# The opening of a two-block transformer kernel: the values' projection in sweeps, its squares summed on VectorE, the constants loaded later, products of ones in front

## The chip, the cores and the metric

The program runs on one core of a Trainium2 chip, as one launch. The metric is the device time of that core in microseconds (us), the median of several runs. The engines are named as the profile names them: PE is TensorE's matrix products and PEld its weight loads, DVE is VectorE, ACT is ScalarE, POOL is GpSimd, SP is SyncE, which here only issues transfers.

## What is computed

Two transformer blocks over 512 tokens of width 1024, one after the other. Cut to what matters here:

```python
# first block; x is (512, 1024)
h = x * rsqrt(mean(x * x, axis=-1) + 1e-6) * pre_norm_g
proj = h @ w_in                      # 3592 columns; v_c are columns 2560 to 3071
q_a, f_a, i_a, g_a, u_b, g_b, q_c, k_c, v_c, g_c, f_c = split(proj)
# a gated recurrence on (q_a, f_a, i_a, g_a), a windowed mean on (u_b, g_b),
# attention with forgetting on (q_c, k_c, v_c, g_c, f_c)
x = x + rmsnorm(concat(o_a, o_b, o_c) @ w_out, post_norm_g)
# second block: two attentions, a merge, an output projection, then a 1024 -> 4096 -> 1024 MLP
```

The root mean square of x is applied after the products: the kernel multiplies the raw x (times the gain) with the weights, and scales the results by token when the sum of squares is there.

## The kernel before

**Two parts of every number.** Each large product is made of three products of rounded numbers. A feature tile x is split into a high part `hh` (ACT, by `enter` at L891) and a low part `hl` (DVE, `enter` at L1294); a weight chunk is split into `wh` (ACT, `hi` at L883) and `wl` (DVE, `lo` at L1289). PE adds hh·wh, hh·wl and hl·wh.

**The stream of weights.** All weights come as chunks of 128 by 1024 in the order of `PLAN`. Each chunk c lands in one of two buffers `raw`, and is split into one of three pairs `wh`, `wl`. SP issues the load of chunk c after `lo(c - 2)` has freed the buffer; `hi(c)` waits until PE is done with chunk c - 3 (`gemm`). The first four chunks, 0 to 3, are the weights of the values v_c (`w1v`), the next is `w1f`, the next two are `w1q`.

**The opening.** SP loads the eight feature tiles in pairs (`load_x`), alternating with chunks 0 and 1, then the constants `con` and `msk`, then chunk 2 and so on. ACT makes for each tile k the high part and, behind it, the square (L894, into `acc` or one of four buffers `S`); POOL adds the squares up into `acc` (L1881), and from tile 5 on ACT's square waits for the addition that frees its buffer. DVE makes the low parts of tiles and chunks in the same order. PE's first program (L457 to L459) takes tile after tile, and in each the four banks `PB0` to `PB3` with three products each: 8 tiles by 4 banks by 3 parts, 96 products of 128 by 512 in all. It waits for `lo` of the chunk and for `xl` of the tile before any of a tile's twelve products. Behind them PE makes the product of chunk 4, in its middle the sums of squares over the partitions (`sums`, L369, four products of one column), and chunks 5 and 6.

**Order on the engines.** The order of every engine is written out by hand in its program. Behind the eight tiles, ACT has a small exponential (L1000) that waits for a DVE operation (L1413), which stands behind all of DVE's low parts of tiles; only then come `hi` and `lo` of chunks 2 to 5. ACT waits for `con` behind `hi(5)`, DVE behind `lo(5)`. The rest of the kernel is driven by PE's progress: its loads and splits are released as PE finishes chunks.

Of the kernel before, what the change touches and what calls it, by code (L numbers as in the profile page):

```python
# [7 lines left out]
F32 = mybir.dt.float32  # L8
# [3 lines left out]
ALU = mybir.AluOpType  # L12
# [29 lines left out]
NW = 1024  # L42
NR, FAR = 2, 8
ORDER1 = (4, 5, 6, 2, 3, 0, 7, 1)

# [118 lines left out]
def build(nc, A, out):  # L164
    with ExitStack() as ctx:
# [144 lines left out]

        SQX = [S[k][:] if k < 4 else ar(12288 + 512 * (k - 4), 512) for k in range(8)]
        half_of = [slice(256 * x, 256 * x + 256) for x in range(2)]
        POST = {1: P_POST1, 2: P_POSTM, 3: P_POSTF}
# [4 lines left out]
        def pe(e):  # L318
# [126 lines left out]


            got = [tenant(m, "vc", m)[0] for m in range(4)]
            for n in range(4):
                c = CH["w1v", n]
                a, b = wh[c % 3], wl[c % 3]  # L450
                e.wait_ge(*to("lo", c))
                for kk in range(2):
                    k = 2 * n + kk
                    w = slice(512 * kk, 512 * kk + 512)
                    e.wait_ge(*to("xl", 0, k))
                    for m in range(4):
                        e.matmul(got[m][:], hh[:, k, col(m)], a[:, w], start=k == 0, stop=False)  # L457
                        e.matmul(got[m][:], hh[:, k, col(m)], b[:, w], start=False, stop=False)
                        i = e.matmul(got[m][:], hl[:, k, col(m)], a[:, w], start=False, stop=k == 7)  # L459
                i.then_inc(*up("gemm", c))  # L460
# [3 lines left out]
            half(c, 0, bank, hh, hl)  # L464
            e.wait_ge(*to("xa", 0, 7))
            sums(0, 5)
# [236 lines left out]
            half(c, 0, bank, hh, hl)  # L703
            e.wait_ge(*to("xs", 7))
            sums(1, 5)
# [171 lines left out]
        def act(e):  # L877
# [7 lines left out]
            def enter(k):  # L885

                if k % 2 == 0:
                    e.wait_ge(semaphore(f"x{k // 2}"), 16)
                if k == 0:
                    e.wait_ge(semaphore("par"), 16)  # L890
                e.activation(hh[:, k, :], X[:, k, :], ACT.Identity, scale=pcol(P_PRE1 + k)).then_inc(*up("xh", 0, k))  # L891
                if k > 4:
                    e.wait_ge(*to("xa", 0, k - 4))
                e.activation(S[k % 4][:] if k else acc[:], X[:, k, :], ACT.Square).then_inc(*up("xq", 0, k))  # L894

# [96 lines left out]
            enter(0)  # L992
            hi(0)
            enter(1)
            enter(2)
            hi(1)
            for k in range(3, 8):
                enter(k)
            e.wait_ge(*to("lb", 0))
            e.activation(lbx[:, 0:2], lbx[:, 0:2], ACT.Exp).then_inc(*up("le"))  # L1000
            for c in range(2, 6):
                hi(c)
            e.wait_ge(semaphore("con"), 16)
# [280 lines left out]
        def dve(e):  # L1284
            def lo(c):
# [4 lines left out]
                                ALU.subtract).then_inc(*up("lo", c))  # L1290

            def enter(k):
                e.wait_ge(*to("xh", 0, k))
                e.scalar_tensor_tensor(hl[:, k, :], X[:, k, :], pcol(P_PRE1 + k), hh[:, k, :].bitcast(F32),  # L1294
                                       ALU.mult, ALU.subtract).then_inc(*up("xl", 0, k))
# [108 lines left out]
            enter(0)  # L1404
            lo(0)
            enter(1)
            enter(2)
            lo(1)
            for k in range(3, 8):
                enter(k)  # L1410

            e.wait_ge(semaphore("par"), 16)
# [8 lines left out]
            e.tensor_scalar(oml, nlb, -1.0, 1.0, ALU.mult, ALU.add).then_inc(*up("lb", 4))  # L1421
            for c in range(2, 6):
                lo(c)
            e.wait_ge(semaphore("con"), 16)
# [250 lines left out]
            for k in range(1, 8):  # L1675
                e.wait_ge(*to("xq", 1, k))
                if k > 1:
                    e.wait_ge(*to("xs", k - 1))
                e.tensor_tensor(acc[:], acc[:] if k > 1 else SQX[0], SQX[k], ALU.add).then_inc(*up("xs", k))
                if k == 3:  # L1680
                    lo(CH["w2e", 2])
# [164 lines left out]
        def pool(e):  # L1846
# [27 lines left out]
            for g in range(4):  # L1874
                r = rows(g % 2)
                e.dma_start(PWM[r, g // 2, rows(g % 2)], A["pool_w"][g]).then_inc(semaphore(f"pw{g}"), 16)
            for k in range(1, 8):
                e.wait_ge(*to("xq", 0, k))
                if k > 1:
                    e.wait_ge(*to("xa", 0, k - 1))  # L1880
                e.tensor_tensor(acc[:], acc[:], S[k % 4][:], ALU.add).then_inc(*up("xa", 0, k))  # L1881

# [96 lines left out]
        def sync(e):  # L1979
# [19 lines left out]
            load_x(2)  # L1999
            load_x(3)  # L2000
            e.dma_start(con[:], A["con"]).then_inc(semaphore("con"), 16)
            e.dma_start(mskw[:], A["msk"]).then_inc(semaphore("msk"), 16)
            for c in range(2, len(PLAN)):
                load(c)
# [139 lines left out]
```

## Time and profile before

| | us |
|---|---|
| median of 3 runs (1023.38 to 1028.22) | 1024.05 |
| profiled execution, its own time | 1029.89 |
| span of the profiled execution | 1028.4 |
| PE busy | 967.5 |
| DVE busy | 593.5 |
| ACT busy | 425.6 |
| POOL busy | 127.4 |

The profiled execution took 1.5 us outside its span, and 5.8 us more than the median of the runs. Starts of PE's instructions are more telling than their durations: a product's row goes on to a modelled end, and the next one starts before that, so the cost of a product in a full stream is the distance between two starts.

### The profile page before, as it was taken

The numbers are of one execution on the slowest core, as the hardware profiler recorded it, in microseconds if no ns is written. First come the engines' busy times: TensorE is split into PE (matmuls) and PEld (weight loads), VectorE is DVE, ScalarE is ACT, GpSimd is POOL, SyncE is SP. The second block draws the span as 40 slices with busy tenths as digits, with TensorE's granted clock in tenths as the row PEclk, the third lists the DMA queues.
The fourth block names the chain that finished last, engine by engine and source line by source line (L and its number), as shares of the span: only waits on it lengthen the run. The fifth ranks groups of instructions, "written<-read, shape, count | busy, mean of one in ns | idle before, by whom it ended". The sixth has DMA issues, their size and how long they took to land.

```text
span 1028.4 us, 13602 instructions
## 1 busy us (share of the span) xinstructions
PE 967.5 (94%) x5210; PEld 781.2 (76%) x5210; DVE 593.5 (58%) x1066; ACT 425.6 (41%) x812; POOL 127.4 (12%) x123
## 2 busy tenths in 40 slices
PE   5998999999999998999998999999989999999992
PEld 4876877767898775766776889978868888888881
DVE  7368558757748676656654752883244344434445
ACT  5354336245465244545544324463233124214321
POOL 6004102321030000000000213030000000000024
PEclk9999999999999999999999999999999999999997
DMA  5221112112233311211212352263323323332002
GB/s 203 98 83 62 42 63 69 56 42 72 83 103 108 139 41 49 70 43 56 82 42 63 101 185 63 82 225 103 101 63 100 103 85 102 103 94 91 21 1 82
DMA packets 24719, 86.72 MB, mean 84 GB/s; under 512 B 2896, under 2 KB 3600, under 8 KB 24400
## 3 DMA queue, kind: packets, MB, share of 16 engines
q1 hardware_dynamic: 23408, 80.25, 24.2%
q10 hardware_dynamic: 1008, 5.28, 1.3%
q8 instruction: 42, 0.69, 0.3%
q0 software_dynamic: 240, 0.33, 0.1%
q14 instruction: 21, 0.17, 0.0%
HBM read 81.65 MB, written 4.19 MB: 83 GB/s over the span
## 4 chain that ended last, share of the span: by engine, by line
PE 80%; DVE 12%; ACT 5%; issue 2%; DMA 0%; POOL 0%; SPq 0%; DVEq 0%; ACTq 0%
PE PB L323 12%; PE PB L325 11%; PE PB L324 11%; PE PB L871 6%; PE PB L870 6%; PE PB L869 6%; PE PB L515 3%; PE PB L542 3%; DVE wl L1289 2%; PE PB L526 2%; PE PB L835 1%; PE PB L354 1%; PE PB L836 1%; PE PB L837 1%; PE PB L355 1%
## 5 line engine op out<-in xcount | busy, mean ns | idle before, releaser
L323 PE MATMUL PB<-hh,wh 128*128 128x512 f32 x592 | 248.8, 420 | 3.5 <-DVE AR L1695 1.9
L325 PE MATMUL PB<-hh,wl 128*128 128x512 f32 x592 | 232.8, 393 | 0.0
L324 PE MATMUL PB<-hl,wh 128*128 128x512 f32 x592 | 232.2, 392 | 0.0
L1289 DVE TENSOR_TENSOR wl<-raw,wh 128x1024 fp32r<-128x1024 f32 (+1 forms) x93 | 119.2, 1283 | 71.1 <-ACT wh L883 71.0
L323 PEld LDWEIGHTS PB<-hh,wh 128*128 128x128 f32 x592 | 112.0, 189 | 36.5 <-issue 12.4
L324 PEld LDWEIGHTS PB<-hl,wh 128*128 128x128 f32 x592 | 112.2, 190 | 24.1 <-issue 3.6
L325 PEld LDWEIGHTS PB<-hh,wl 128*128 128x128 f32 x592 | 111.7, 189 | 24.7
L883 ACT ACTIVATE wh<-raw 128x1024 fp32r<-128x1024 f32 (+1 forms) x93 | 94.5, 1019 | 62.2 <-PE PB L837 14.2
L1033 ACT ACTIVATE S<-S,sm 128x256 f32<-128x256 f32 (+3 forms) x96 | 50.8, 530 | 129.1 <-DVE sm L1374 92.3
L871 PE MATMUL PB<-gh,wl 128*128 128x512 f32 x256 | 99.6, 389 | 0.0
L869 PE MATMUL PB<-gh,wh 128*128 128x512 f32 x256 | 99.6, 389 | 0.0
L870 PE MATMUL PB<-gl,wh 128*128 128x512 f32 x256 | 99.6, 389 | 0.0
L1289 DVE TENSOR_TENSOR wl<-AR,wh 128x1024 fp32r<-128x1024 f32 x56 | 69.4, 1239 | 47.3 <-ACT wh L883 47.3
L883 ACT ACTIVATE wh<-AR 128x1024 fp32r<-128x1024 f32 x56 | 58.9, 1051 | 67.9 <-PE PB L871 67.9
L1812 DVE TENSOR_TENSOR tmp<-tmp 128x512 f32<-128x512 f32 x32 | 23.2, 725 | 82.1 <-ACT gh L1249 82.1
L1860 POOL TENSOR_TENSOR acc<-acc,tmp 128x512 f32<-128x512 f32 x14 | 19.8, 1414 | 329.4 <-ACT tmp L1274 298.6
L1245 ACT ACTIVATE tmp<-PB 128x512 f32<-128x512 f32 x32 | 19.1, 596 | 95.0 <-PE PB L325 92.8
L869 PEld LDWEIGHTS PB<-gh,wh 128*128 128x128 f32 x256 | 48.0, 188 | 10.0
L870 PEld LDWEIGHTS PB<-gl,wh 128*128 128x128 f32 x256 | 48.0, 188 | 10.0
L871 PEld LDWEIGHTS PB<-gh,wl 128*128 128x128 f32 x256 | 48.0, 188 | 9.9
L1374 DVE CUSTOM_DVE_ANT_0 S<-PB,MK 128x128 f32<-128x128 f32 (+3 forms) x64 | 29.8, 489 | 37.7 <-PE PB L515 37.1
L1835 DVE TENSOR_TENSOR AR<-PB,AR 128x512 f32<-128x512 f32 x24 | 16.6, 692 | 60.5 <-PE PB L871 60.5
(337 smaller groups left out, 1669.5 us busy)
## 6 DMA issues: line engine op xcount, KB each, us to landing
AR<-in_dne SPq DMA_DIRECT2D x32, 512.0 KB, 3.5
AR<-in_upe SPq DMA_DIRECT2D x24, 512.0 KB, 3.5
raw<-in_w2g SPq DMA_DIRECT2D x16, 512.0 KB, 3.4
raw<-in_w1e SPq DMA_DIRECT2D x10, 512.0 KB, 3.4
raw<-in_w1q SPq DMA_DIRECT2D x8, 512.0 KB, 3.5
raw<-in_woab SPq DMA_DIRECT2D x8, 512.0 KB, 3.5
raw<-in_w2e SPq DMA_DIRECT2D x6, 512.0 KB, 3.8
X<-in_xT SPq DMA_DIRECT2D x4, 512.0 KB, 6.5
```

Source lines behind the costliest of these rows:

```text
L323: e.matmul(bank[:], a[:, col(k)], xa[:, k, :], start=k == 0, stop=False)
L324: e.matmul(bank[:], a[:, col(k)], xb[:, k, :], start=False, stop=False)
L325: i = e.matmul(bank[:], b[:, col(k)], xa[:, k, :], start=False, stop=k == 7)
L515: last = e.matmul(bank[b][:, k], query[b], key[b][:, k], start=a == 2, stop=x == parts - 1)
L542: x = e.matmul(bank[rows(b), col(i)], v, PT[b][:, j - lo, :], start=j == lo, stop=j == i)
L869: e.matmul(bank[:], a[:, col(k)], gh[:, k, :], start=k == 0, stop=False)
L870: e.matmul(bank[:], a[:, col(k)], gl[:, k, :], start=False, stop=False)
L871: i = e.matmul(bank[:], b[:, col(k)], gh[:, k, :], start=False, stop=k == 7)
L883: e.activation(wh[c % 3][:, 0:PLAN[c][2]], raw_of(c), ACT.Copy).then_inc(*up("hi", c))
L1033: e.activation(s, s, ACT.Exp, bias=nm, scale=-1.0, accum_out=su).then_inc(*up("exp", a, n, b))
L1289: e.tensor_tensor(wl[c % 3][:, 0:n], raw_of(c), wh[c % 3][:, 0:n].bitcast(F32), ALU.subtract).then_inc(*up("lo", c))
L1374: e.tensor_tensor_reduce(soft(n, b)[:, 0:w], seat["max", a, n, b][:, 0:w], MK[:, T - w:T], -1.0, BIG, ALU.add, ALU.min, scalars(n, b)[0]). ...
```

## The change

The change touches the first thirty-odd microseconds.

- PE starts with fourteen products of `ones` by `ones` (128 by 128, not rounded numbers) into bank 7, as soon as `ones` is written.
- For each tile the twelve products of the values are made in three sweeps over the four banks: first hh·wh, then hl·wh, then hh·wl. The first sweep waits for the two high parts only, the second for the tile's low part, the third for the chunk's low part. The number of these products stays 96.
- Chunk 0 is split in two halves of 512 columns, one for each of its tiles (`first_half` on ACT and DVE).
- ACT makes the high parts of tiles 0 to 7 and of chunks 0 to 2 without squares between them; the squares of tiles 0 to 3 come behind `hi(2)`, those of tiles 4 to 7 behind `hi(3)`, each into a buffer of its own (`SQ0`).
- The seven additions of squares move from POOL to DVE, three behind `lo(2)` and four behind `lo(3)`.
- `hi(2)`, `hi(3)`, `lo(2)` and `lo(3)` move ahead of the small exponential and what goes with it.
- SP issues chunks 2 and 3 ahead of `con` and `msk`.

```diff
@@ pe
+            e.wait_ge(*to("one"))
+            for _ in range(WARM):                      # WARM = 14
+                e.matmul(PB[7][:, 0:128], ones[:], ones[:], start=True, stop=True)
             for n in range(4):
-                e.wait_ge(*to("lo", c))
                 for kk in range(2):
+                    e.wait_ge(*to("xh", 0, k))
+                    e.wait_ge(*(to("hi", c) if n else to("hi", 0, kk)))
+                    for m in range(4):
+                        e.matmul(got[m][:], hh[:, k, col(m)], a[:, w], start=k == 0, stop=False)
                     e.wait_ge(*to("xl", 0, k))
                     for m in range(4):
-                        e.matmul(got[m][:], hh[:, k, col(m)], a[:, w], start=k == 0, stop=False)
-                        e.matmul(got[m][:], hh[:, k, col(m)], b[:, w], start=False, stop=False)
-                        i = e.matmul(got[m][:], hl[:, k, col(m)], a[:, w], start=False, stop=k == 7)
+                        e.matmul(got[m][:], hl[:, k, col(m)], a[:, w], start=False, stop=False)
+                    e.wait_ge(*(to("lo", c) if n or kk else to("lo", 0, 0)))
+                    for m in range(4):
+                        i = e.matmul(got[m][:], hh[:, k, col(m)], b[:, w], start=False, stop=k == 7)
@@ act
             enter(0)
-            hi(0)
             enter(1)
+            first_half(0)
+            first_half(1)
             enter(2)
+            enter(3)
             hi(1)
-            for k in range(3, 8):
+            for k in range(4, 8):
                 enter(k)
+            hi(2)
+            for k in range(4):
+                square0(k)
+            hi(3)
+            for k in range(4, 8):
+                square0(k)
             e.wait_ge(*to("lb", 0))
             e.activation(lbx[:, 0:2], lbx[:, 0:2], ACT.Exp).then_inc(*up("le"))
-            for c in range(2, 6):
-                hi(c)
+            hi(4)
+            hi(5)
+            def first_half(x):                         # the one of ACT; dve's is its low part
+                if x == 0:
+                    e.wait_ge(*landed(0))
+                w = slice(512 * x, 512 * x + 512)
+                e.activation(wh[0][:, w], raw_of(0)[:, w], ACT.Copy).then_inc(*up("hi", 0, x))
+            def square0(k):
+                e.activation(SQ0[k], X[:, k, :], ACT.Square).then_inc(*up("xq", 0, k))
@@ dve
+            def added_x(k0, k1):
+                for k in range(k0, k1):
+                    e.wait_ge(*to("xq", 0, k))
+                    if k > 1:
+                        e.wait_ge(*to("xs", 0, k - 1))
+                    e.tensor_tensor(acc[:], acc[:] if k > 1 else SQ0[0], SQ0[k], ALU.add).then_inc(*up("xs", 0, k))
@@ pool
-            for k in range(1, 8):
-                e.wait_ge(*to("xq", 0, k))
-                if k > 1:
-                    e.wait_ge(*to("xa", 0, k - 1))
-                e.tensor_tensor(acc[:], acc[:], S[k % 4][:], ALU.add).then_inc(*up("xa", 0, k))
@@ sync
+            load(2)
+            load(3)
             e.dma_start(con[:], A["con"]).then_inc(semaphore("con"), 16)
             e.dma_start(mskw[:], A["msk"]).then_inc(semaphore("msk"), 16)
-            for c in range(2, len(PLAN)):
+            for c in range(4, len(PLAN)):
                 load(c)
```

On PE, the first rows of its program; before, the first half of the first tile's twelve rows (of the two operands named, the second is the one that is held):

```order
L457 MATMUL PB0<-wh0,hh 128x512
L458 MATMUL PB0<-wl0,hh 128x512
L459 MATMUL PB0<-wh0,hl 128x512
L457 MATMUL PB1<-wh0,hh 128x512
L458 MATMUL PB1<-wl0,hh 128x512
L459 MATMUL PB1<-wh0,hl 128x512
```

Of the change, the same place:

```order
L451 MATMUL PB7<-ones 128x128 x14
L464 MATMUL PB0<-wh0,hh 128x512
L464 MATMUL PB1<-wh0,hh 128x512
L464 MATMUL PB2<-wh0,hh 128x512
L464 MATMUL PB3<-wh0,hh 128x512
L467 MATMUL PB0<-wh0,hl 128x512
L467 MATMUL PB1<-wh0,hl 128x512
L467 MATMUL PB2<-wh0,hl 128x512
L467 MATMUL PB3<-wh0,hl 128x512
L470 MATMUL PB0<-wl0,hh 128x512
```

The first product that needs a chunk's low part is the ninth of a tile now, where it was the second; fourteen products of ones stand ahead.

On DVE, from the low part of chunk 1 on, before (`hl` are low parts of tiles, `wl` those of chunks, the rows on `sm` belong to the small exponential):

```order
L1289 TENSOR_TENSOR wl1<-raw1,wh1 128x1024
L1294 SCALAR_TENSOR_TENSOR hl<-X,par,hh 128x512 x5
L1413 TENSOR_TENSOR sm<-par 128x2
L1415 RECIPROCAL sm<-sm 128x2
L1417 TENSOR_TENSOR sm<-sm 128x2
L1419 TENSOR_TENSOR sm<-sm 128x2
L1421 TENSOR_SCALAR sm<-sm 128x2
L1289 TENSOR_TENSOR wl2<-raw0,wh2 128x1024
```

Of the change, the same place:

```order
L1315 TENSOR_TENSOR wl1<-raw1,wh1 128x1024
L1333 SCALAR_TENSOR_TENSOR hl<-X,par,hh 128x512 x4
L1315 TENSOR_TENSOR wl2<-raw0,wh2 128x1024
L1329 TENSOR_TENSOR acc<-S0,S1 128x512
L1329 TENSOR_TENSOR acc<-acc,S2 128x512
L1329 TENSOR_TENSOR acc<-acc,S3 128x512
L1315 TENSOR_TENSOR wl0<-raw1,wh0 128x1024
L1329 TENSOR_TENSOR acc<-acc,AR 128x512 x4
L1458 TENSOR_TENSOR sm<-par 128x2
```

The low part of chunk 2 comes right behind the last four of the eight tiles, that of chunk 3 behind three additions, and the rows on `sm` behind all seven additions.

## Rows read from the trace of the kernel before

**Rows 1.** The page: busy time, share of the span and instructions of each engine.

```profile
PE 967.5 (94%) x5210; PEld 781.2 (76%) x5210; DVE 593.5 (58%) x1066; ACT 425.6 (41%) x812; POOL 127.4 (12%) x123
```

**Rows 2.** Stages: busy time in each, the granted clock (PEclk), DMA share, GB/s.

```profile
core 0: us, PE busy (x) PEld busy (x) DVE busy (x) ACT busy (x) POOL busy (x), PEclk, DMA share, GB/s
20.00:25.00 5.00, 1.93 (x9) 1.29 (x8) 4.44 (x8) 2.10 (x3) 0.87 (x1) 0.99 0.02 6
25.00:30.00 5.00, 5.00 (x16) 3.94 (x15) 1.29 (x2) 1.06 (x1) 0.00 (x0) 0.67 0.62 204
```

**Rows 3.** Timeline of PE: start, duration, engine, line, out<-in, idle before.

```profile
8.38 0.79 PE L457 MATMUL PB<-wh,hh 128*128 128x512 f32 x1 [8.38 <-DVE wl L1289]
8.98 0.63 PE L458 MATMUL PB<-wl,hh 128*128 128x512 f32 x1
...
11.11 0.47 PE L457 MATMUL PB<-wh,hh 128*128 128x512 f32 x1
...
20.53 0.39 PE L459 MATMUL PB<-wh,hl 128*128 128x512 f32 x1
23.99 0.50 PE L457 MATMUL PB<-wh,hh 128*128 128x512 f32 x1 [3.07 <-DVE wl L1289]
...
28.43 0.40 PE L457 MATMUL PB<-wh,hh 128*128 128x512 f32 x1
...
36.38 0.39 PE L459 MATMUL PB<-wh,hl 128*128 128x512 f32 x1
36.60 0.39 PE L323 MATMUL PB<-hh,wh 128*128 128x512 f32 x1
```

**Rows 4.** Timeline of DVE and POOL in the same stretch.

```profile
5.46 0.75 DVE L1294 SCALAR_TENSOR_TENSOR hl<-X,par,hh 128x512 fp32r<-128x512 f32 x1 [4.45 <-ACT hh L891]
7.11 1.23 DVE L1289 TENSOR_TENSOR wl<-raw,wh 128x1024 fp32r<-128x1024 f32 x1 [0.90 <-ACT wh L883]
8.29 12.58 POOL L1881 TENSOR_TENSOR acc<-acc,S 128x512 f32<-128x512 f32 x7 [1.76 <-ACT S L894]
10.61 2.31 DVE L1289 TENSOR_TENSOR wl<-raw,wh 128x1024 fp32r<-128x1024 f32 x1
12.84 8.58 DVE L1294 SCALAR_TENSOR_TENSOR hl<-X,par,hh 128x512 fp32r<-128x512 f32 x5
```

**Rows 5.** Timeline of ACT in the same stretch.

```profile
4.70 0.72 ACT L891 ACTIVATE hh<-X,par 128x512 fp32r<-128x512 f32 x1 [2.20 <-DMA X<-in_xT]
5.33 0.61 ACT L894 ACTIVATE acc<-X 128x512 f32<-128x512 f32 x1
6.02 1.06 ACT L883 ACTIVATE wh<-raw 128x1024 fp32r<-128x1024 f32 x1
21.53 0.20 ACT L1000 ACTIVATE sm<-sm 128x2 f32<-128x2 f32 x1 [5.57 <-DVE sm L1413]
21.64 1.99 ACT L883 ACTIVATE wh<-raw 128x1024 fp32r<-128x1024 f32 x2
```

**Rows 6.** DMA issues up to 70 us: count, KB each, median us to landing.

```profile
X<-in_xT SPq DMA_DIRECT2D x4, 512.0 KB, 6.5
raw<-in_w1v SPq DMA_DIRECT2D x4, 512.0 KB, 5.6
con<-in_con SPq DMA_DIRECT2D x1, 662.5 KB, 9.5
```

**Rows 7.** The chain that ended last, its piece ahead of the first split of a chunk.

```profile
1.24 4.76 DMA raw<-in_w1v
```

**Rows 8.** Timeline of PE: weight loads and products of numbers that are not rounded.

```profile
39.10 1.08 PEld L369 LDWEIGHTS PB<-ones,acc 128*128 128x128 f32 x8
39.32 0.95 PE L369 MATMUL PB<-ones,acc 128*128 128x1 f32 x8
```

**Rows 9.** Timeline of PE in a later projection with a wait ahead of each sweep.

```profile
259.74 1.07 PE L359 MATMUL PB<-gl,wh 128*128 128x512 f32 x4
260.65 0.39 PE L354 MATMUL PB<-gh,wh 128*128 128x512 f32 x1
```

**Rows 10.** A later stage with a fallen clock, columns as in rows 2.

```profile
80.00:100.00 20.00, 17.13 (x130) 13.01 (x128) 16.94 (x30) 8.34 (x20) 9.89 (x12) 0.91 0.21 73
```

**Rows 11.** The page: the additions of 128 by 512 with both inputs in memory on DVE.

```profile
L1812 DVE TENSOR_TENSOR tmp<-tmp 128x512 f32<-128x512 f32 x32 | 23.2, 725 | 82.1 <-ACT gh L1249 82.1
```

More of the change, by code:

```diff
@@ L43 @@
 NR, FAR = 2, 8
+WARM = 14
 ORDER1 = (4, 5, 6, 2, 3, 0, 7, 1)
@@ L311, in build @@
         SQX = [S[k][:] if k < 4 else ar(12288 + 512 * (k - 4), 512) for k in range(8)]
+        SQ0 = [S[k][:] if k < 4 else ar(2048 + 512 * (k - 4), 512) for k in range(8)]
         half_of = [slice(256 * x, 256 * x + 256) for x in range(2)]
@@ L464, in pe @@
             half(c, 0, bank, hh, hl)
-            e.wait_ge(*to("xa", 0, 7))
+            e.wait_ge(*to("xs", 0, 7))
             sums(0, 5)
@@ L703, in pe @@
             half(c, 0, bank, hh, hl)
-            e.wait_ge(*to("xs", 7))
+            e.wait_ge(*to("xs", 1, 7))
             sums(1, 5)
@@ L891, in enter @@
                 e.activation(hh[:, k, :], X[:, k, :], ACT.Identity, scale=pcol(P_PRE1 + k)).then_inc(*up("xh", 0, k))
-                if k > 4:
-                    e.wait_ge(*to("xa", 0, k - 4))
-                e.activation(S[k % 4][:] if k else acc[:], X[:, k, :], ACT.Square).then_inc(*up("xq", 0, k))
+            def first_half(x):
[5 more added lines that the diff above has]
+                e.activation(SQ0[k], X[:, k, :], ACT.Square).then_inc(*up("xq", 0, k))
             def enter_half(s, k, x):
@@ L1290, in lo, with first_half @@
                                 ALU.subtract).then_inc(*up("lo", c))
+            def first_half(x):
+                w = slice(512 * x, 512 * x + 512)
+                e.wait_ge(*to("hi", 0, x))
+                e.tensor_tensor(wl[0][:, w], raw_of(0)[:, w], wh[0][:, w].bitcast(F32),
+                                ALU.subtract).then_inc(*(up("lo", 0) if x else up("lo", 0, 0)))
+            def added_x(k0, k1):
[4 more added lines that the diff above has]
+                    e.tensor_tensor(acc[:], acc[:] if k > 1 else SQ0[0], SQ0[k], ALU.add).then_inc(*up("xs", 0, k))
             def enter(k):
@@ L1404, in dve @@
             enter(0)
-            lo(0)
+            first_half(0)
             enter(1)
+            first_half(1)
             enter(2)
+            enter(3)
             lo(1)
-            for k in range(3, 8):
+            for k in range(4, 8):
                 enter(k)
+            lo(2)
+            added_x(1, 4)
+            lo(3)
+            added_x(4, 8)
             e.wait_ge(semaphore("par"), 16)
@@ L1421, in dve @@
             e.tensor_scalar(oml, nlb, -1.0, 1.0, ALU.mult, ALU.add).then_inc(*up("lb", 4))
-            for c in range(2, 6):
-                lo(c)
+            lo(4)
+            lo(5)
             e.wait_ge(semaphore("con"), 16)
@@ L1677, in dve @@
                 if k > 1:
-                    e.wait_ge(*to("xs", k - 1))
-                e.tensor_tensor(acc[:], acc[:] if k > 1 else SQX[0], SQX[k], ALU.add).then_inc(*up("xs", k))
+                    e.wait_ge(*to("xs", 1, k - 1))
+                e.tensor_tensor(acc[:], acc[:] if k > 1 else SQX[0], SQX[k], ALU.add).then_inc(*up("xs", 1, k))
                 if k == 3:
```

## The prediction, made before the changed kernel was run

> **What bounds the kernel now.** I read the page first. PE is busy for 94% of the span [rows 1], and no other engine for more than 58%, so an opening is worth what PE gets earlier through it, provided that nothing behind it takes the time back. The timeline of PE then shows what the opening costs. The first of the 96 products of the values starts at 8.38, and the next program starts at 36.60 [rows 3]: 28.22 us. What they need at full speed is read from the undisturbed end: from 28.43 to 36.38 there are 35 steps, 7.95 us, so 0.227 us each, and 96 make 21.8 us. The opening therefore loses 28.2 - 21.8 = 6.4 us after its start, in three places:
>
> - the first six products, from 8.38 to 11.11, take 2.73 us where six steps of 0.227 take 1.36: 1.4 us. Their distance of about 0.43 (8.98 and the rows behind it) is that of half the clock;
> - a wait from 20.76 (20.53 and one step) to 23.99, 3.2 us, for the low part of chunk 2 [rows 3];
> - behind this wait the clock falls. The stage 25 to 30 has a granted clock of 0.67 [rows 2], which is a part at 1.2 GHz and the rest at 2.4, after a stage 20 to 25 in which PE worked for 1.93 of 5 us. Eight products from 25.09 to 28.43 take 3.34 us instead of 1.8: 1.5 us.
>
> The rest, 0.3, is small stretches. Why is chunk 2 late? ACT starts the high part of chunk 2 at 21.64 because it stands behind a small exponential, which waited 5.57 us for DVE [rows 5]. DVE stands at low parts of tiles that take 8.58 us for five [rows 4], 1.72 each, where the one at 5.46 took 0.75. Over the same time POOL adds squares, 12.58 us for seven. Alternating, the two engines slow each other: DVE's low part of chunk 1 also takes 2.31 instead of 1.23.
>
> **The change part by part.** I lay out the new opening with these durations, and clock times of this execution.
>
> *Start of the real products.* The first tile is there at 4.70 as before. ACT makes two high parts of tiles, with 0.63 from start to start (4.70 to 5.33 [rows 5]), so until about 6.0. Chunk 0 lands at 1.24 + 4.76 = 6.00 [rows 7], no earlier than ACT is free. Half of its high part costs what a row of 512 does, 0.61 [rows 5]; with it done at 6.65 the first sweep can start at 6.7. Before, a full high part (1.06) and a full low part (1.23 [rows 4]) stood ahead: 8.38. Gain 1.7. Where the first sweep ends, at 7.6, the tile's low part has been there since about 6.2, and where the second ends, at 8.5, the half low part of chunk 0 (6.7 plus some 0.7) has been there for a us.
>
> *Do the later products find their data?* At full speed a tile takes 2.72 us, so tile k begins at 6.7 + 2.72 k. ACT needs 0.63 for each high part and 1.06 for a chunk, with the landings in between. The transfers of x take 3.9 to 8.3 us, with 6.5 as the median [rows 6], and x pair 1, chunk 1, x pairs 2 and 3 follow each other on one queue; the last is issued at 3.2, so it lands at about 11.5. From that: high parts of tiles 2 and 3 by 8.8 (PE wants the first at 12.2), chunk 1 by 9.9 (wanted 12.2), tiles 4 to 7 by 12.9 (wanted from 17.6), chunk 2 by 14.5 (wanted 17.6, the tightest, 3 us of cover), four squares of 0.62, chunk 3 by 17.5 (wanted 23.1), four squares by 20. On DVE, with 0.75 for each tile and 1.23 for a chunk: chunk 1 by 12 (wanted by the third sweep at 14.0), chunk 2 by 16 (wanted 19.4), three additions of 0.73 [rows 11], chunk 3 by 19, four additions by 21, which PE wants in the middle of chunk 4, after 30. So no wait of 3.2 and, as the wait was what preceded it, no fallen clock of 1.5.
>
> *The moved adds* cost DVE 7 x 0.73 = 5.1 us, less than the 5 x (1.72 - 0.75) + (2.31 - 1.23) = 5.9 that it gets back from POOL's absence; and none of them stands ahead of `lo(2)`.
>
> *The loads.* With chunks 2 and 3 ahead of `con`, `con` is issued behind `lo(1)`, at about 12 instead of 3.8, and takes 9.5 or less [rows 6], so it lands by 21.5. ACT and DVE ask for it behind chunk 5, for whose buffer PE must be at 23; if that cover were gone, each us of delay would cost a us.
>
> *More waits on PE*, three for each tile instead of one. In the later projection with a wait ahead of each sweep, four products of a sweep take from 259.74 to 260.65 [rows 9], 0.228 each: satisfied waits cost nothing.
>
> *The products of ones.* Each is two weight loads and two products in the records: the four with one column have 8 rows, 1.08 us of loads [rows 8], so 0.135 at most per pair at full speed. Fourteen are 28 pairs, 3.8 us at the full clock and 7.6 at half. Started at about 1.1 they end between 4.9 and 8.7; if the half clock lasts 2.7 us as it did from 8.38 on, ten pairs are done in it and eighteen take 2.4: they end at 6.2, before the data. So the likeliest cost is nothing, and the gain is the 1.4 us of slow products. At the other bound, all at half the clock, real products begin 2.0 us late and may still be slow for their first ones.
>
> The Trainium skill ("FP8 and Floating Point Precision", on true FP32) has four passes through the array for such numbers. By that alone fourteen of 128 columns would be worth fourteen of 512 columns, and as a by-sum 14 x 0.227 = 3.2 us at the full clock, 6.4 at half: an end between 4.3 and 7.5, which would bring the late bound down to 0.8 us.
>
> **Sum.** 1.7 (earlier start) + 1.4 (slow first products) + 3.2 (wait) + 1.5 (fallen clock) + 0.3 = 8.1 us: the next program starts at 6.7 + 21.8 = 28.5 instead of 36.6. I take 0.6 off, between nothing and the 2.0 of the late bound, for the products of ones and a clock that is not up at once. 7.5 us. All that follows is released by PE's progress, so it shifts as a whole. Against its own time the profiled execution goes from 1029.9 to 1022.4. It was 5.8 us slower than the median; from the median the same 7.5 us give **1016.5 us**, -0.73%. What a measurement of this kernel can tell from no change is about 0.5%, 5.1 us, as its three runs lie 4.8 us apart.
>
> **Rivals.**
>
> *The clock is not up when the real products begin* (chance 15%). The products of ones run into the data: real ones start 2 us late, and the first of them are slow, 1.4. Gain 8.1 - 3.4 = 4.7, or about 1019.3. For it: the load rate of [rows 8] is for one execution, and nothing shows it at half the clock. Against: PE began at 8.38 with nothing in front of it and was up by 11.11.
>
> *The wait moves instead of going* (10%). DVE remains the late engine, as the additions now stand on it, or ACT is late with chunk 2. The Trainium skill ("Perfetto Trace Analysis", on scalar and DVE operations) warns that moving work between GpSimd and DVE might not help, since they share a read port. As a mechanism here: had the additions cost DVE what POOL's cost it, DVE would be no earlier, a wait of some 3 us would stay and with it the slow products behind it, 1.5: gain 8.1 - 4.7 = 3.4, 1020.6. Against it: 0.75 against 1.72 in [rows 4], and the order, `lo(2)` before any addition.
>
> *Slower: the clock falls more often behind.* There are five later stages of 20 us with a mean clock of 0.91, such as 80 to 100 [rows 10], each behind a pause of PE, and each worth about 1.5 us as above. Other pauses of one to three us passed without it. With the whole kernel shifted, pauses meet the clock's control at another moment. Five more falls would eat the gain, nine more would make it 0.5% slower (13 us, over 1029). It speaks against that, that pauses are as long as before, and that three runs spread over only 4.8 us, some three falls. 3%.
>
> *No effect* (7%): something behind the opening that doesn't hang on PE sets the time, and takes most of it back; the loads of the next chunks would be the place. Within 2 us of 1024. Against: between 28 and 70 us SP's loads are issued as chunks are freed. The forecast itself has 65%, with 1013.5 to 1018.7 as its own range (at best 8.1 gained and 2.4 from falls of the clock that stay away, at worst 5.3 gained).
>
> **Range and chances.** The first two rivals lie at 1019.3 and 1020.6, so the range goes to 1021, and down to 1012.5 for one or two falls fewer: 8 in 10. Faster by over 0.5% (below 1018.9): most of the forecast, 62%, nearly half of the first rival, some of the second, and with the falls either way about 0.74; within 0.5%: 0.21; slower 0.05.
>
> **What would show it.** Right: products of ones from about 1.1; first real product at 6.7 with 0.227 between starts; no idle time until the end of the values at 28.5; DVE's low parts at 0.75; no stage with a clock below 1 before 80 us. Wrong: real products 0.43 apart after 7; PE waiting for `wh` or `wl` of chunk 2; the start of L325's first product, the former L323, later than 30.5; or an early start there and a span that is no shorter.

## The result, and the profile of the changed kernel

| | before | changed |
|---|---|---|
| median, us | 1027.02 (1023.38 to 1028.69, 15 runs) | 1021.17 (1016.40 to 1022.85, 15 runs) |
| ratio (95% interval) | | 0.9945 (0.9928 to 0.9963) |
| profiled execution: own time, span | 1029.89, 1028.4 | 1020.96, 1019.7 |
| start of the first product behind the values | 36.60 | 28.64 |

The change takes 5.85 us off the median (0.55% by the ratio), where 7.5 us and 0.73% were forecast, and 1021.17 stands where 1016.5 was forecast, just above the end of the forecast range at 1021. The spans of the two profiled executions lie 8.7 us apart, of which the opening makes 7.96.

The timeline of PE in the changed kernel (start, duration, engine, line, out<-in, idle before) answers to [rows 3]:

```profile
1.06 5.92 PE L451 MATMUL PB<-ones 128*128 128x128 f32 x28 [1.06 <-DVE ones L1442]
6.79 1.16 PE L464 MATMUL PB<-wh,hh 128*128 128x512 f32 x4
7.79 1.07 PE L467 MATMUL PB<-wh,hl 128*128 128x512 f32 x4
8.69 1.07 PE L470 MATMUL PB<-wl,hh 128*128 128x512 f32 x4
...
19.57 1.07 PE L470 MATMUL PB<-wl,hh 128*128 128x512 f32 x4
...
27.73 1.07 PE L470 MATMUL PB<-wl,hh 128*128 128x512 f32 x4
28.64 0.39 PE L325 MATMUL PB<-hh,wh 128*128 128x512 f32 x1
```

The first real product starts at 6.79, and the sweeps follow each other every 0.91 us, four products of 0.227, with no idle time in brackets down to 28.64. The wait of [rows 3] for chunk 2 is gone, and so are the slow first products of the values: what runs slowly now are the products of ones. DVE, against [rows 4]:

```profile
8.55 1.41 DVE L1333 SCALAR_TENSOR_TENSOR hl<-X,par,hh 128x512 fp32r<-128x512 f32 x2
9.88 1.22 DVE L1315 TENSOR_TENSOR wl<-raw,wh 128x1024 fp32r<-128x1024 f32 x1
11.01 2.73 DVE L1333 SCALAR_TENSOR_TENSOR hl<-X,par,hh 128x512 fp32r<-128x512 f32 x4
13.88 1.23 DVE L1315 TENSOR_TENSOR wl<-raw,wh 128x1024 fp32r<-128x1024 f32 x1
15.03 0.68 DVE L1329 TENSOR_TENSOR acc<-S 128x512 f32<-128x512 f32 x1
15.82 1.49 DVE L1329 TENSOR_TENSOR acc<-acc,S 128x512 f32<-128x512 f32 x2
17.23 1.22 DVE L1315 TENSOR_TENSOR wl<-raw,wh 128x1024 fp32r<-128x1024 f32 x1
18.36 3.08 DVE L1329 TENSOR_TENSOR acc<-acc,AR 128x512 f32<-128x512 f32 x4
```

A tile's low part takes 0.68 (2.73 for four) instead of 1.72. The low part of chunk 2 is done at 15.1 (13.88 + 1.23), and the first sweep that needs it starts at 19.57. The additions take 5.25 us, 5.1 were forecast. ACT, against [rows 5]:

```profile
6.01 1.15 ACT L909 ACTIVATE wh<-raw 128x512 fp32r<-128x512 f32 x2
...
12.80 1.05 ACT L894 ACTIVATE wh<-raw 128x1024 fp32r<-128x1024 f32 x1
...
15.84 1.05 ACT L894 ACTIVATE wh<-raw 128x1024 fp32r<-128x1024 f32 x1
...
24.42 0.19 ACT L1030 ACTIVATE sel<-con 128x8 fp32r<-128x8 f32 x1
```

The high part of chunk 2 is made at 12.80 instead of 21.64, and ACT takes up `con` at 24.42 with no idle time in front. The issues of SP up to 70 us (KB each, median us to landing) give `con` 5.1 us instead of the 9.5 of [rows 6]:

```profile
con<-in_con SPq DMA_DIRECT2D x1, 662.5 KB, 5.1
```

So the opening came out as laid out, 28.64 against a forecast 28.5. What is left between it and the end is the granted clock. Each stretch below 1.00 lasts about 3.4 us and lies at 0.50, the lower of the clock's two levels, 1.2 GHz. (One more, behind PE's last product, lasts to the end of the span, 13 to 17 us in each profile of the whole kernels; no product runs in it, so it costs nothing, but it lowers the mean clock of an execution.) The first in the changed kernel, in windows of one us (busy time of PE, PEld, DVE, ACT, POOL; granted clock; DMA share; GB/s):

```profile
194.00:195.00 1.00, 0.75 (x6) 0.78 (x8) 1.00 (x3) 0.00 (x0) 0.00 (x0) 0.55 0.00 0
195.00:196.00 1.00, 1.00 (x14) 1.00 (x10) 0.21 (x1) 0.75 (x3) 0.05 (x1) 0.50 0.07 16
196.00:197.00 1.00, 1.00 (x6) 0.68 (x4) 0.67 (x2) 0.97 (x2) 1.00 (x1) 0.50 0.00 0
197.00:198.00 1.00, 1.00 (x5) 0.82 (x4) 0.96 (x5) 0.97 (x3) 0.23 (x1) 0.74 0.00 0
```

It stands behind a pause of PE of 2.28 us, and the first product of the next projection, at 196.26, takes 0.59 to the next start instead of 0.23:

```profile
194.25 2.08 PE L578 MATMUL PB<-AR 64*128 64x128 f32 x16 [2.28 <-DVE AR L1525]
196.26 0.79 PE L325 MATMUL PB<-hh,wh 128*128 128x512 f32 x1
196.85 0.63 PE L326 MATMUL PB<-hl,wh 128*128 128x512 f32 x1
```

I call such a stretch a fall. The profiled execution of before has six, one of them in the opening ([rows 2]), that of the changed kernel has four, near 194, 340, 545 and 743.

The slow start of an execution is not in this column. In the changed kernel it reads 1.00 in the first stretches too:

```profile
0.00:5.00 5.00, 3.94 (x18) 3.94 (x19) 0.17 (x1) 1.59 (x2) 4.47 (x14) 1.00 0.58 203
5.00:10.00 5.00, 5.00 (x26) 4.48 (x25) 4.07 (x7) 4.52 (x7) 1.52 (x3) 1.00 1.04 396
```

Half speed there is read from the distance between starts alone: 0.213 for a record of the products of ones, against 0.12 later, and about 0.43 for a product of 512 columns, against 0.227. In a fall, where the column says 0.50, the distance is 0.43 as well.

### The profile page after: what moved, and what is told of

Its sections match the earlier page's. It is cut to its first block, busy times and chain, and to the rows that moved or that the text cites. A ratio compares the mean times of both kernels' runs of the same rounds, so it can differ in the third digit from the quotient of the medians.

```text
span 1019.7 us, 13664 instructions
## 1 busy us (share of the span) xinstructions
PE 968.7 (95%) x5238; PEld 784.6 (77%) x5238; DVE 591.1 (58%) x1074; ACT 426.1 (42%) x813; POOL 116.6 (11%) x116
## 4 chain that ended last, share of the span: by engine, by line
PE 80%; DVE 12%; ACT 5%; issue 3%; POOL 0%; DVEq 0%; ACTq 0%
PE PB L325 11%; PE PB L327 11%; PE PB L326 11%; PE PB L881 6%; PE PB L882 6%; PE PB L880 6%; PE PB L526 3%; PE PB L553 3%; DVE wl L1315 2%; PE PB L537 2%; PE PB L846 1%; PE PB L847 1%; PE PB L356 1%; PE PB L848 1%; PE PB L357 1%
## 5 line engine op out<-in xcount | busy, mean ns | idle before, releaser
L1315 DVE TENSOR_TENSOR wl<-raw,wh 128x1024 fp32r<-128x1024 f32 (+2 forms) x92 | 117.6, 1278 | 64.5 <-ACT wh L894 64.2
L894 ACT ACTIVATE wh<-raw 128x1024 fp32r<-128x1024 f32 (+2 forms) x92 | 93.5, 1018 | 56.4 <-PE PB L848 14.7
```

What stands on the lines that cost most here:

```text
L894: e.activation(wh[c % 3][:, 0:PLAN[c][2]], raw_of(c), ACT.Copy).then_inc(*up("hi", c))
L1315: e.tensor_tensor(wl[c % 3][:, 0:n], raw_of(c), wh[c % 3][:, 0:n].bitcast(F32), ALU.subtract).then_inc(*up("lo", c))
```

## The experiments

Two theories stood at the start. By the first (G in the expectations) the opening is worth the 8 us seen between the two profiled executions, and falls behind it give part back. By the rival (F) the opening was worth less from the start, since the profiled execution of before was one of its slow ones. Two more theories, P and O, are about the wait for chunk 2: P blames POOL's additions beside DVE's low parts, O the place of chunk 2 behind the exponential. Falls were counted in the same way in every profile.

**Before, once more.** No edit.

> The kernel before, unchanged, for the spread of its runs and a second profile. Theory F (falls): the time of an execution is a fixed time plus about 1.55 us for each stretch of 3.4 us at 1.2 GHz, and the moment at which PE's pauses meet the clock's control differs from run to run. Then the runs stand in steps: spans near 1022.5 at a mean clock of 0.987, up to 1027.5 at 0.983, and the opening of this profile has another length than 28.2 us (with or without the fall at 25, with another length of slow first products). Theory G (given back): the opening is 28.2 us long in this profile too, within 0.3, and the spread comes from behind it alone.

Measured: 1026.98 us (1023.98 to 1031.74, 12 runs), ratio 1.0014 (0.9996 to 1.0032). The spans of the runs gather near 1022.5, 1024.1, 1027.0, 1028.6 and 1030, within 0.4 us. PE's timeline:

```profile
8.60 0.80 PE L457 MATMUL PB<-wh,hh 128*128 128x512 f32 x1 [8.60 <-DVE wl L1289]
...
13.03 0.60 PE L458 MATMUL PB<-wl,hh 128*128 128x512 f32 x1
...
24.21 0.50 PE L457 MATMUL PB<-wh,hh 128*128 128x512 f32 x1 [2.14 <-DVE wl L1289]
24.55 0.40 PE L458 MATMUL PB<-wl,hh 128*128 128x512 f32 x1
...
35.22 0.39 PE L323 MATMUL PB<-hh,wh 128*128 128x512 f32 x1
```

The same program, another execution: the slow first products last until 13, not 11, the wait ends at the same 24.2, is 2.14 long instead of 3.07, and no fall follows it. The next program starts at 35.22. So the 1.5 us of [rows 3] behind the wait are there in one of these two executions and not in the other, and the opening of the changed kernel is 6.6 us shorter than this one.

**Without the products of ones.**

```diff
-WARM = 14
+WARM = 0
```

> The changed kernel without the fourteen products of ones. By the prediction's own term for slow first products the loss is 1.4 us, now paid by real products from 6.7 on. By the profile of the changed kernel, where the clock came up 5.3 us after PE's start, it could be up to 2.7 us (5.3 us at half speed). If the products of ones bring nothing, the time is that of the changed kernel, 1021.2 within 1.

Measured: 1019.01 us (1018.67 to 1023.85, 6 runs), ratio 0.9939 (0.9918 to 0.996). The profile has slow products from 6.73 to about 12.8 and its next program at 31.43, 2.8 us later than in the changed kernel. The median shows none of it, and is even 2.2 us lower: five of these six runs have a mean clock of 0.990 or more, and twelve of the changed kernel's fifteen have 0.985 or less. Runs of the same mean clock can be compared. At 0.990 and 0.991 four runs without the ones have spans of 1017.3 to 1017.5 (a fifth has 1018.7), and the three of the changed kernel at 0.990 have 1015.0 to 1015.2: 2.3 us apart.

**Before with the products of ones, and with its wait filled.** Fourteen products in front; in the second kernel ten more ahead of the wait for chunk 2.

```diff
+            for _ in range(14):
+                e.matmul(PB[7][:, 0:128], ones[:], ones[:], start=True, stop=True)
...
+                if n == 2:
+                    for _ in range(10):
+                        e.matmul(PB[7][:, 0:128], ones[:], ones[:], start=True, stop=True)
```

> The kernel before with only the fourteen products of ones in front. They end at 7.0, 1.4 us ahead of the first real product. If a clock that is up stays up over this pause, 1.4 to 2.7 us less than before. If the slow first products are only moved, no change. No effect on the wait for chunk 2.

> As e3, and ten products of ones ahead of the wait for the low part of chunk 2, where PE would stand idle for 3.1 us; the order of all else is that of before. Theory F: this takes away the fall of the clock behind that wait in every execution and nothing else, so it lies under e3 by 1.55 us times the share of runs that had it: 0 to 1.5. The wait itself stays: PE gets to chunk 4 at about 33.8 where before had 36.6. If the fall is not caused by the pause, nothing changes against e3.

Measured: 1028.66 us (1025.54 to 1031.75, and one outlier, 12 runs), ratio 1.0012 (0.9997 to 1.0028); and 1027.33 (1025.58 to 1030.34, 12 runs), 1.0012 (0.9998 to 1.0027). Neither gains, though 1.4 to 2.7 us were expected of the first if the clock stayed up over the pause, as it did in its profile. The first kernel's PE:

```profile
1.06 6.09 PE L449 MATMUL PB<-ones 128*128 128x128 f32 x28 [1.06 <-DVE ones L1407]
8.32 0.50 PE L461 MATMUL PB<-wh,hh 128*128 128x512 f32 x1 [1.17 <-DVE wl L1293]
8.66 0.40 PE L462 MATMUL PB<-wl,hh 128*128 128x512 f32 x1
...
23.93 0.79 PE L461 MATMUL PB<-wh,hh 128*128 128x512 f32 x1 [4.44 <-DVE wl L1293]
24.52 0.63 PE L462 MATMUL PB<-wl,hh 128*128 128x512 f32 x1
```

The real products run at the full clock from the first on, and PE merely arrives sooner at the wait, which ends at 23.93 and is 4.44 us long, with a fall behind it. In the order of before, chunk 2's low part comes at 24 whatever PE does (23.99, 24.21, 23.93), so the 1.4 us of slow first products are covered by that wait. The second kernel's PE:

```profile
1.06 5.40 PE L449 MATMUL PB<-ones 128*128 128x128 f32 x28 [1.06 <-DVE ones L1410]
8.40 0.55 PE L464 MATMUL PB<-wh,hh 128*128 128x512 f32 x1 [1.94 <-DVE wl L1296]
...
21.04 2.39 PE L457 MATMUL PB<-ones 128*128 128x128 f32 x20
24.00 0.50 PE L464 MATMUL PB<-wh,hh 128*128 128x512 f32 x1 [0.57 <-DVE wl L1296]
24.34 0.40 PE L465 MATMUL PB<-wl,hh 128*128 128x512 f32 x1
```

With the wait filled there is no fall at 24. One came instead near 8.7, behind a pause of 1.94 us. The opening ends at 35.01, 1.6 us earlier than in the first profile of before, but six falls stand behind it where that one had five, and the spans are about equal (1028.7 and 1028.4).

**The openings alone.** Both kernels end behind chunk 6, by a few lines of early ends in each engine's program, and write x out.

> The kernel before, ended behind chunk 6 (the second w1q): all engines stop there and the eight rows of x are written out unchanged, so nothing of the blocks is in the output. Its time is the opening's and what lies around it. Theory F: runs stand in two groups 1.4 us apart (with and without a fall of the clock behind the wait for chunk 2); how slow the first products are does not show, since the wait for chunk 2 ends at about 24.0 whatever PE did before. Mean gain of the cut changed kernel against it: 6.6 to 8.0. Theory G (the opening gains 8 in every run and 2 us are given back behind it): a difference of 8.0.

> The changed kernel, ended at the same place and in the same manner. Theory F: its runs vary with the moment at which the clock comes up (from 2.7 to 6 us behind PE's start): up to about 1.5 us later where the products of ones run at half speed to their end and the first real ones do too; the mean gain against the cut kernel before is then 5.5 to 7.5, and the measured 5.9 of the whole kernels needs nothing given back. Theory G: all runs alike, 8.0 under the cut kernel before.

Measured: 62.01 us (61.98 to 62.35, 5 runs) and 55.69 (55.59 to 55.76, 4 runs). The opening cut out is worth 6.32 us, and each of the two kernels spreads over less than 0.4. That is not theory G's 8.0. For theory F it is below the 6.6 to 8.0 of the first expectation and inside the 5.5 to 7.5 of the second. The two groups of runs, 1.4 us apart, that F gave are not there: the runs of the first kernel stand at 61.98 to 62.35, and its profile shows no fall at 25. How often executions of the whole kernel before have that fall is not known, beyond one of its two profiles. In the first kernel the wait for chunk 2 reads:

```profile
23.31 2.36 DVE L1294 TENSOR_TENSOR wl<-raw,wh 128x1024 fp32r<-128x1024 f32 x2 [0.18 <-ACT wh L884]
...
24.59 0.50 PE L457 MATMUL PB<-wh,hh 128*128 128x512 f32 x1 [2.45 <-DVE wl L1294]
```

Three parts of the change were then taken back, one at a time, in the cut changed kernel: no products of ones; the additions on POOL, behind its memsets, from the buffers `SQ0`; and the twelve products of a tile in the old order, with both low parts waited for first.

```diff
-WARM = 14
+WARM = 0
```

```diff
+            for k in range(1, 8):                      # pool, as dve's added_x before
+                e.wait_ge(*to("xq", 0, k))
+                e.tensor_tensor(acc[:], acc[:] if k > 1 else SQ0[0], SQ0[k], ALU.add).then_inc(*up("xa", 0, k))
```

```diff
+                    e.wait_ge(*(to("lo", c) if n or kk else to("lo", 0, 0)))
+                    e.wait_ge(*to("xl", 0, k))
+                    for m in range(4):                 # hh.wh, hh.wl, hl.wh for each bank
```

> The cut changed kernel (e6) without the products of ones; like e6 it stops behind chunk 6 and writes x out. In e2 the next program started at 31.4 where the changed kernel had 28.6. If products of ones count in the changed order, where PE never waits, this is 1.4 to 2.8 us over e6: 57.1 to 58.5. If they count as little as in the order of before (e3 against before: nothing), 55.7.

> The cut changed kernel with the seven additions of squares back on POOL, the squares still made late and into buffers of their own; stops behind chunk 6, writes x out. Theory P (POOL's additions beside DVE's low parts are what made chunk 2 late): they now run from 14 to 22 beside lo(2), lo(3) and nothing before, so part of the slowing comes back, but chunk 3 has 4 us of cover: 55.7 to 56.2. Theory O (the order is what counts, hi(2) and lo(2) ahead of squares and exponential): 55.7, no difference.

> The cut changed kernel with PE in the old order, three products for each bank, behind waits for both low parts (chunk 0 still in halves); stops behind chunk 6, writes x out. The sweeps are worth the time from the half high part to the half low part of chunk 0, 0.7 us, if nothing else waits: 56.4. If the sweeps hid waits of later tiles too, 57 or more.

Measured: 58.00 us (57.57 to 58.51, 4 runs), 55.72 (55.67 to 55.77) and 56.56 (56.38 to 56.59). In the changed order the products of ones are worth 2.3 us, the sweeps 0.9, and the engine of the additions nothing: the squares now come when DVE has made all of its tiles' low parts. POOL still slows DVE where they meet, the low part of chunk 3 takes 1.87 us beside it instead of 1.22, but nothing waits for it.

From the other side, three edits were made in the cut kernel of before: the seven additions on DVE behind the low part of chunk 3 (with the squares in buffers of their own, so that ACT no longer waits for an addition); `hi` and `lo` of chunks 2 and 3 ahead of the small exponential; the products of ones.

```diff
+            lo(2)                                      # dve
+            lo(3)
+            for k in range(1, 8):
+                e.wait_ge(*to("xq", 0, k))
+                e.tensor_tensor(acc[:], acc[:] if k > 1 else SQ0[0], SQ0[k], ALU.add).then_inc(*up("xs", 0, k))
```

```diff
+            hi(2)                                      # act, and lo(2), lo(3) in dve
+            hi(3)
             e.wait_ge(*to("lb", 0))
```

> The cut kernel before (e5) with the additions of squares taken from POOL and made by DVE behind lo(3), squares in buffers of their own; PE's order, the exponential's place and the loads as before; stops behind chunk 6, writes x out. Theory P (POOL beside DVE is what made chunk 2 late): DVE's low parts of tiles end near 17 instead of 21.4, chunk 2 is ready near 19, PE never waits for it: 3 us under e5 less what the slow first products now cost, 59.0 to 60.5. Theory O (the place behind the exponential counts): no more than 1 us under e5, 61 to 62.

> The cut kernel before with hi(2), hi(3), lo(2), lo(3) moved ahead of the small exponential and nothing else; POOL still adds; stops behind chunk 6, writes x out. DVE's low parts still end at 21.4, then lo(2) at once instead of 1.3 us later: 60.7, 1.3 under e5, by theory P. By theory O most of the 3.1 us: 59 to 59.5.

> The cut kernel before with the fourteen products of ones in front; stops behind chunk 6, writes x out. The wait for chunk 2 ends at 24.0 whatever PE did before, so the time is that of e5, 62.0, or up to 1.4 more where the longer pause now lets the clock fall. By the forecast's sum 1.4 less: 60.6.

Measured: 58.87 us (58.42 to 59.04, 4 runs), 3.1 less than the cut kernel of before; 60.65 (60.58 to 60.83), 1.4 less; and for the ones 62.09, 63.31, 63.46 and 65.22 in four runs, the best of them equal to the 62.01 of the cut kernel of before. The profile of the last kernel, of its slowest run, has a fall from about 10.3, behind a pause of 1.81 us, and two in a row from 24 on, behind the wait; up to 1.4 us more had been expected for one fall, and 3.2 were measured for three. Without POOL beside it, DVE's low part of a tile takes 0.75, and that of chunks 2 and 3 begins at 17.80 instead of 23.31, so no product waits for it (theory P):

```profile
15.76 0.75 DVE L1298 SCALAR_TENSOR_TENSOR hl<-X,par,hh 128x512 fp32r<-128x512 f32 x1 [0.38 <-ACT hh L893]
...
17.80 2.36 DVE L1293 TENSOR_TENSOR wl<-raw,wh 128x1024 fp32r<-128x1024 f32 x2 [0.19 <-ACT wh L885]
```

The order of chunk 2 alone shortens the wait from 2.45 to 1.16 us:

```profile
22.86 0.50 PE L457 MATMUL PB<-wh,hh 128*128 128x512 f32 x1 [1.16 <-DVE wl L1296]
```

With POOL out of the way no wait is left that it could shorten. So 3.1 us of the opening come from taking the additions away from the early low parts, which removes the wait, and 3.2 from the rest of the change. Taken back singly, the ones account for 2.3 of that and the sweeps for 0.9. That these add up to 3.2 need not mean that nothing else counts, since the parts can overlap, and the halves of chunk 0 were not taken back alone.

**Fills in later pauses.** The changed kernel, and that of before with both fills of above, with products of ones also ahead of six later waits (`fill` makes n products into a bank that is written anew behind them). The second version fills five of the waits, leaves out the one at 206, has four or six products for each, and puts those for the wait at 75 ahead of the right step.

```diff
+            def fill(bank, t, n):
+                for _ in range(n):
+                    e.matmul(bank[:, t], ones[:], ones[:], start=True, stop=True)
...
+                if (a, n) in ((1, 1), (2, 31)):        # first version: (1, 3), 7 products
+                    fill(bank, col(i), 6)
                 e.wait_ge(*to("pta", a, n))
```

> The changed kernel with 5 to 10 products of ones in each of six later pauses of PE (ahead of the waits that ended at 75.2, 113.1, 194.3, 206.1, 545.4 and 743.5 in its profile). Results are not touched; the products write a bank part that is overwritten. Theory F: falls are caused by these pauses, so at most one or two of them stay (the pause at 339.8 is not filled), the runs lie closer together, and the time is under the changed kernel by 1.6 us for each fall taken away, two to four of them: 1014.5 to 1018. If sparse products don't hold the clock, or the falls don't come from pauses, the time is 1021 or up to 1 us more.

> The kernel before with the same products in the later pauses, with the fourteen in front and the ten in the wait for chunk 2. Theory F: falls are rare in both, so the difference between this and e7 is that of the openings without a fall, 35.0 - 28.6 = 6.4 us, with less spread than between the plain kernels. Theory G: 8 us in the openings and 2 given back: also about 6 here, but then e5 and e6 lie 8 apart.

> As e7, with the faults of its fills mended: six products ahead of the wait at 75 (they stood ahead of another step and cost about 3 us), four at 113, none at 206, where the products themselves waited, six at 194, 545 and 743. e7 had one fall of the clock and 3 us of products in the way. Theory F: one to three falls, nothing in the way, 1.65 us for each fall less than the changed kernel's four: 1015.5 to 1018.5. If a fall costs less than 1.65, or the fills cost more than the pauses hide, 1019 to 1021.

Measured: 1021.21 us (1019.5 to 1023.07, 6 runs), ratio 0.9942 (0.9927 to 0.9958); 1026.91 (1025.27 to 1029.94, 12 runs), 0.9994 (0.9982 to 1.0005); 1018.10 (1016.12 to 1018.17, 6 runs), 0.9921 (0.9898 to 0.9943). The first version missed its 1014.5 to 1018: its profile has one fall, near 76, but the products of ones stand in the way of real ones. Behind the opening it needs 989.51 us with one fall, where the changed kernel in its second profile, below, needs 986.56 with one: 2.95 us more, against the 4.5 that three falls less save. Before with the same fills is 5.7 us slower than it, where theory F gave 6.4. In the second, the pause at 194 is filled, and the one at 204.68 is not:

```profile
191.89 1.50 PE L323 MATMUL PB<-ones 128*128 128x128 f32 x12
194.34 0.90 PE L588 MATMUL PB<-AR 64*128 64x128 f32 x11 [0.94 <-DVE AR L1537]
...
204.68 0.81 PE L599 MATMUL PB<-con,AR 128*128 128x128 f32 x3 [2.22 <-ACT early L1147]
205.14 0.77 PE L329 MATMUL PB<-hh,wh 128*128 128x512 f32 x1
205.71 0.63 PE L330 MATMUL PB<-hl,wh 128*128 128x512 f32 x1
```

Windows around these and the other pauses, columns as above:

```profile
60.00:100.00 40.00, 38.22 (x299) 31.73 (x298) 32.72 (x64) 21.83 (x48) 12.64 (x14) 1.00 0.19 64
190.00:203.00 13.00, 11.52 (x84) 8.88 (x82) 8.42 (x19) 4.08 (x8) 2.04 (x2) 1.00 0.13 40
203.00:206.00 3.00, 1.32 (x5) 1.22 (x6) 2.91 (x6) 2.12 (x6) 0.00 (x0) 0.81 0.19 22
...
339.00:346.00 7.00, 6.09 (x24) 5.16 (x25) 3.51 (x7) 0.87 (x3) 0.27 (x1) 0.76 0.22 75
540.00:550.00 10.00, 8.86 (x69) 7.42 (x66) 4.22 (x6) 4.69 (x6) 0.00 (x0) 1.00 0.18 54
735.00:750.00 15.00, 13.52 (x63) 10.59 (x62) 6.55 (x12) 4.77 (x8) 0.00 (x0) 1.00 0.15 47
```

Its two falls stand behind the two pauses of over 1.9 us that were left open, 204.68 (2.22) and 339.91 (1.94); the filled stretches, at 60 to 100, 190 to 203, 540 and 735, stay at 1.00.

**The changed kernel, once more**, beside before, in another session.

> The changed kernel, unchanged, for its steps beside a count of the falls in a second profile. Spans at 1013.5 plus 1.55 for each fall: 1015.0, 1019.7 and 1021.3 as before; the opening ends between 28.6 and 29.2. Median against before 0.994 within 0.002.

Measured: 1016.50 us (1016.40 to 1017.54, 4 runs) beside 1026.93 (7 runs), ratio 0.9899 (0.9885 to 0.9914), not the expected 0.994 within 0.002. The start behind the values is at 28.64 again; the profile has one fall, near 740, and a span of 1015.2. Three of the first fifteen runs of the changed kernel had stood on this step too.

## Why the prediction was off

The median is 4.67 us above the forecast. 1.65 of them are gain that did not come (5.85 for 7.5), and 3.0 are the level from which the forecast started (1027.02 for 1024.05).

**What a fall costs.** The span behind the opening (span less the start of the next program) against the falls in it:

| profile | opening ends | falls behind it | rest |
|---|---|---|---|
| changed, once more | 28.64 | 1 | 986.56 |
| before, once more | 35.22 | 3 | 988.48 |
| changed | 28.64 | 4 | 991.06 |
| changed, no ones | 31.43 | 4 | 990.97 |
| before | 36.60 | 5 | 991.80 |
| before, wait filled | 35.01 | 6 | 993.69 |
| before, ones in front | 36.45 | 6 | 993.75 |

Two of the six in each of the last two rows follow each other without a gap (6.8 us at 0.50 from about 200 on). From one to four falls in the changed kernel the rest grows by 4.5 us, 1.5 each, and before's spans, over all sessions, gather 1.5 to 1.6 apart (1022.5, 1024.1, 1025.6, 1027.2). 1.5 was forecast. Profiles with the same count agree within 0.1 us here; with 1.5 taken off for each fall, all lie between 984.0 and 985.1, and what makes this last 1 us is open.

**Point by point.**

- *Start of the real products*: 6.79 for 6.7. Right.
- *Data for the later products, the moved additions, the later constants, the waits ahead of each sweep*: no idle time of PE from 6.79 to 28.64. Right, the constants with more room than thought.
- *The products of ones*: 5.92 us, ending at 6.98 by their modelled end, for a likeliest 6.2. Half speed, by the distance of the starts, lasted until about 6.3, 5.3 us where I had taken over 2.7, and yet the end met the data. The Trainium skill ("FP8 and Floating Point Precision", on true FP32) has four passes, which gave 6.4 at half the clock as an estimate; measured are records 0.213 apart at half the clock, so 5.96 for 28, and at the full clock ten products in 2.39 us, where the same estimate gives 2.27. The trace agrees with it within 7%.
- *The rival of the shared port* (the wait moves instead of going) fell: DVE's additions cost 0.75, and the low parts 0.68. The Trainium skill ("Perfetto Trace Analysis", on scalar and DVE operations) says that GpSimd and DVE share a read port. The kernel before agrees with it: a low part took 1.72 beside POOL and 0.75 with the additions away. That the slowing comes from POOL is shown; that the port is its cause no run here can tell.
- *The sum*. **This is the step that failed.** "1.7 + 1.4 + 3.2 + 1.5 + 0.3 = 8.1" added up what one execution had lost, and it does so rightly: the two profiled openings lie 7.96 apart. But I took it for what every execution loses ("from the median the same 7.5 us"). The term of 1.5, the fall behind the wait, is absent in the second profile of before and in the cut kernel. The term of 1.4 isn't one of its own either: a longer slow start shortens the wait, since that ends at 24 in any case. The opening cut out is worth 6.3 us; the median moved by 5.85.
- *The level*. The other 3 us of the miss are in the starting value: 1024.05 was the median of three runs of a time that moves in steps of 1.5 from 1023.4 to 1028.7, and fifteen runs gave 1027.02. I had read the spread of "some three falls" as a bound on a rival and not as doubt about the median. 1027.02 - 6.3 is 1020.7. In the last session the changed kernel ran at 1016.50, the very forecast. That is luck: before stood at 1026.93 beside it, 2.9 above the level of the forecast, so the gain there was 10.4 and not 7.5.
- *Falls behind the opening* were a rival on the slow side with 3%, and "one or two falls fewer" in the range on the fast side. The pauses that "passed without it" in the first profile were of up to 2.22 us and not of up to three: both pauses above 2.4 behind the opening, 2.48 and 3.17, had a fall. Falls weigh more than 3%, on both sides: the same changed kernel had four falls in one profile and one in another, with ratios of 0.9945 and 0.9899 in the two sessions, whose intervals don't meet. 6.3 us alone would be 0.9939.

**What stays open.** Why the number of falls differs. The pauses of the changed kernel are equally long in both of its profiles (2.33 at 75, 1.89 at 113, 2.28 at 194, 2.22 at 205, 1.94 at 340, 2.5 at 545, 3.2 at 743), and four or one of them were followed by a fall. That filling a pause keeps its fall away is borne out by the profiles: the longest of them, 3.2 us near 743, has a fall behind it in all seven profiles without fills behind the opening, and in none of the three with them. That the filled kernel is faster than the changed one isn't shown, as 0.9921 lies between the changed kernel's own two ratios. The effect of the loads' order alone wasn't tried.

## What to carry to other kernels

A profile prices one execution: before its stalls are added up, profile the same kernel twice and cut the stretch out as a kernel of its own, whose runs here agreed within 0.4 us for both kernels (within 1 without the products of ones), where the whole kernels' spread over 5. A speed-up ahead of a wait that something else ends is worth nothing until that wait goes, so ask of each term where the next wait ends without it. And keep an engine that adds off the stretch in which DVE is the late one; later on its place made no difference.

## What the runs showed that was not expected

- By the distance of the starts, full speed came 5.3 us after PE's first product in the changed kernel, 2.7 us after it in the profile of before, 4.9 in its second profile (8.60 to about 13.5), and 6.1 in the changed kernel without the ones (6.73 to about 12.8), with PE busy throughout.
- The falls cost about 1.5 us each, wherever they come. Each of those seen stands behind a pause of PE of 1.8 us or more (1.81 in the cut kernel with ones, 1.89 near 123 in the profile of before), or directly behind another fall, and none behind the pauses of 1.0 to 1.6. But a long pause does not always bring one: in the changed kernel one came behind 1.94 us, while pauses of up to 2.33 in the same execution, and of 2.5 in its other profile, passed without.
- Execution times of this kernel therefore gather on steps of 1.5 us, and the most frequent step can differ between sessions: 1019.7 and 1021.3 for the changed kernel's spans in the first, 1015.0 in the last.
